# The head 0 preparation, one tile of the LRU products and the copies of the meta query's scores, moved in a hybrid encoder block on one core

## The reference

```
h = concat(meta (16 tokens), x (1024 tokens))            # T = 1040, D = 1024
proj = rmsnorm(h) @ w_in                                 # x_lru 512, g_lru 512, c_q 256, c_kv 128, k_pe 32
y_lru = rg_lru_bidir(dwconv(x_lru)) * gelu(g_lru)
q, k, v from c_q, c_kv, k_pe                             # 8 heads, QK = 96, V = 64, rmsnorm and rope
y_mla = softmax(q k^T / sqrt(96)) v                      # all 1040 keys
h = h + concat(rmsnorm(y_lru), rmsnorm(y_mla)) @ w_out
h = h + (silu(dwconv(gate)) * up) @ w_ffn_down           # gate, up = rmsnorm(h) @ w_ffn_up, D_FF = 2816
return h[:, 16:]
```

## Time and profile before

| what | value |
|---|---|
| median of 3 runs | 1298.33 us (1298.2 to 1304.07) |
| the profiled execution's own time | 1303.02 us |
| its span | 1301.2 us |
| TensorE busy | 1271.2 us, 98% of the span |
| VectorE busy | 996.9 us, 77% |
| ScalarE busy | 769.3 us, 59% |
| chain that ended last, by engine | PE 85%, DVE 6%, ACT 5%, issue 2%, DMA 1% |

### The profile page before, as it was taken

One profiled execution on the slowest core, in us unless ns is written; L12 is line 12 of the kernel. 1 busy time (PEld: TensorE's weight loads), 2 busy tenths in 40 slices (PEclk: granted clock), 3 DMA queues, 4 the chain that ended last, 5 costly groups with the idle time before them and its releaser, 6 DMA issues.

```text
span 1301.2 us, 18506 instructions
## 1 busy us (share of the span) xinstructions
PE 1271.2 (98%) x6158; PEld 1018.6 (78%) x6158; DVE 996.9 (77%) x1505; ACT 769.3 (59%) x1156; POOL 146.6 (11%) x175
## 2 busy tenths in 40 slices
PE   7999999899999999999999999999999999999998
PEld 7999997666666666687678888888888888888886
DVE  6677569678887876577779887887878887887855
ACT  7487648567765866534445565656474565656460
POOL 3000037400000001322200000000010000000010
PEclk9999999999999999999999999999999999999999
DMA  6111200000000014200144846576574847576667
GB/s 220 34 53 41 74 1 1 1 1 10 9 9 10 9 58 155 69 30 1 49 148 94 187 100 166 118 169 134 151 169 93 189 97 169 113 170 133 157 143 245
DMA packets 40938, 123.01 MB, mean 95 GB/s; under 512 B 7378, under 2 KB 8082, under 8 KB 34484
## 3 DMA queue, kind: packets, MB, share of 16 engines
q0 software_dynamic: 7200, 52.43, 21.4%
q1 hardware_dynamic: 33684, 69.86, 15.7%
HBM read 62.34 MB, written 59.80 MB: 94 GB/s over the span
## 4 chain that ended last, share of the span: by engine, by line
PE 85%; DVE 6%; ACT 5%; issue 2%; DMA 1%; POOL 0%; SPq 0%; DVEq 0%; ACTq 0%
PE banks L2911 30%; PE banks L2983 14%; PE banks L100 7%; PE banks L102 7%; PE banks L101 7%; PE banks L1935 2%; PE banks L2040 2%; PE banks L2041 2%; PE banks L2042 2%; PE banks L2060 2%; PE banks L2063 2%; PE banks L2061 2%; ACT e_f L1558 1%; PE banks L1895 1%; ACT e_h L1565 1%
## 5 line engine op out<-in xcount | busy, mean ns | idle before, releaser
L2911 PE MATMUL banks<-x_hi,slot_h 128*128 128x512 f32 x616 | 242.8, 394 | 2.5 <-DVE slot_l L2599 1.3
L2911 PE MATMUL banks<-x_lo,slot_h 128*128 128x512 f32 x616 | 243.4, 395 | 0.0
L2911 PE MATMUL banks<-x_hi,slot_l 128*128 128x512 f32 x616 | 242.9, 394 | 0.0
L2384 ACT ACTIVATE slot_h<-up_raw 128x512 fp32r<-128x512 f32 x127 | 79.8, 629 | 174.4 <-PE banks L2911 172.3
L2911 PEld LDWEIGHTS banks<-x_hi,slot_h 128*128 128x128 f32 x616 | 115.6, 188 | 30.9 <-DVE slot_l L2599 2.1
L2911 PEld LDWEIGHTS banks<-x_lo,slot_h 128*128 128x128 f32 x616 | 115.7, 188 | 27.1
L2911 PEld LDWEIGHTS banks<-x_hi,slot_l 128*128 128x128 f32 x616 | 115.7, 188 | 26.9
L2462 ACT ACTIVATE staged<-banks 128x1024 f32<-128x1024 f32 x100 | 101.4, 1026 | 41.0 <-PE banks L2983 41.0
L2983 PE MATMUL banks<-dn_h,a_h 128*128 128x512 f32 x280 | 110.4, 394 | 0.0
L2983 PE MATMUL banks<-dn_h,a_l 128*128 128x512 f32 x280 | 109.5, 391 | 0.0
L2983 PE MATMUL banks<-dn_l,a_h 128*128 128x512 f32 x280 | 109.5, 391 | 0.0
(11 more groups left out here) (346 smaller groups left out, 2861.5 us busy)
## 6 DMA issues: line engine op xcount, KB each, us to landing
down_sums<-staged POOLq DMA_DIRECT2D x50, 1024.0 KB, 8.0
...
```

The source lines that it names most:

```text
L2384: nc.scalar.activation(s_h[slot], x, ACT.Copy).then_inc(sem["up_hi"], 1)
L2911: ins = nc.tensor.matmul(o, s[slot][:, k], xs[w], start=fresh and k == 0 and n == 0, stop=k == 3 and n == 2, skip_group_check=not fresh)
```

## The change

- **Head 0's jobs.** `FIRST` packs the 23 jobs ahead of slot 0 in six steps, in a new order (`tq0`, `tk0`, `tq1`, `tk1`, `a0` to `a7`, and only then `tm`). They get eight banks by a list (`side_banks`). Each job waits only for the token tiles it reads (`HEAD_0`). The identity matmuls come ahead of a job and not behind it, and their numbers change: 1 at each of `a0` to `a15` becomes 2 from `a2` on, 6 at `a0`; 10 behind `tk0` become 10 spread over the four transposes; 8 behind `am` become 2 ahead of `r`.
- **Slots 0 and 1 of head 0.** `scores_ahead` computes the scores of both without the row of maxima, and adds the row's product as four matmuls of one row once it has come. In the two slots, where the pv of later slots stands, `keep_busy(8)` issues identity matmuls, 8 for each half.
- **Meta query.** VectorE copies `x0`, `x1`, `x2` out of PSUM, and ScalarE does not. In heads 0 to 6 they stand in slots 1, 2 and 4 (for head 0 they were ahead of slot 0, for heads 1 to 6 in slots 1, 1 and 2); those of head 7 move from slots 4, 5 and 6 of head 6 to slots 5, 6 and 8. SyncE issues `x_one` to `x_all` behind `recip_row` instead of ahead of it, in heads 0 to 6.
- **LRU tile.** The products of tile 4 run between the last pv of full key tiles and the meta pv of head 7. VectorE adds tile 4 ahead of two splits of weights, tile 5 ahead of two others, and tile 6 behind the multiplication of head 7's output; ScalarE splits tiles 6 and 7 earlier.

```diff
     LAST_AHEAD = dict(PREPARE)
-    LAST_AHEAD.update({4: ("a5", "x0", "a6", "a7"), 5: ("a8", "x1", "a9", "a10"), 6: ("a11", "x2", "a12", "a13")})
-    FIRST = dict(PREPARE)
-    FIRST.update({8: ("x0", "x1", "x2", "")})
-    OWN = {1: ("", "", "x0", "x1"), 2: ("", "x2", "", "")}
+    LAST_AHEAD.update({5: ("a8", "x0", "a9", "a10"), 6: ("a11", "x1", "a12", "a13"), 8: ("x2", "", "", "")})
+    FIRST = {0: ("tq0", "tk0", "tq1", "tk1"), 1: ("a0", "a1", "a2", "a3"), 2: ("a4", "a5", "a6", "a7"),
+             3: ("tm", "a8", "a9", "a10"), 4: ("a11", "a12", "a13", "a14"), 5: ("a15", "am", "r", "")}
+    OWN = {1: ("", "", "x0", ""), 2: ("", "x1", "", ""), 4: ("", "x2", "", "")}
...
             if h:
                 recip_row(sp, h - 1)
+            if h != END:
+                last_queries()
...
             if h == HEADS and s == 2:
+                split_y("L", 6)
                 read_output(h)
...
             if (h, s) == (HEADS, 1):
+                add_lru(L_GAP)
                 split_w(4)
                 split_w(5)
-                add_lru(4)
...
+            elif kind in ("x0", "x1", "x2"):
...
+                if c == 0:
+                    if h:
+                        dve.wait_ge(sem["x_in"], 16 * h)
...
+                ins = nc.vector.tensor_copy(x_one[:, 512 * c:512 * c + w], side[0:2, 0:w])
...
-        WARM = {"tk0": 10, "am": 8}
-        WARM.update({f"a{n}": 1 for n in range(2 * XT)})
+        WARM = {"tq0": 2, "tk0": 2, "tq1": 4, "tk1": 2, "a0": 6, "r": 2}
+        WARM.update({f"a{n}": 2 for n in range(2, 2 * XT)})
...
+        def scores_ahead():
+
+            pe.wait_ge(sem["b_set"], 2 + len(LOWS))
+            for g in range(2):
+                ks = slice(P * g, P * g + P)
+                for c in range(2):
+                    cs = slice(512 * c, 512 * c + 512)
+                    out = s_ps(g)[:, cs]
+                    nc.tensor.matmul(out, k_h[0][0:QK, ks], q_h[0][0:QK, cs], start=True, stop=False)
+                    nc.tensor.matmul(out, k_h[0][0:QK, ks], q_l[0][:, cs], start=False, stop=False)
+                    nc.tensor.matmul(out, k_l[0][:, ks], q_h[0][0:QK, cs], start=False, stop=False)
+            pe.wait_ge(sem["row_in"], 16)
+            for g in range(2):
+                for c in range(2):
+                    cs = slice(512 * c, 512 * c + 512)
+                    ins = nc.tensor.matmul(s_ps(g)[:, cs], k_h[0][QK:QK + 1, P * g:P * g + P], q_h[0][QK:QK + 1, cs],
+                                           start=False, stop=True)
+                ins.then_inc(sem["s_done"], 1)
+
+        def keep_busy(n):
+
+            for _ in range(n):
+                nc.tensor.matmul(bank(5)[:, 0:P], ident, ident, start=True, stop=True)
...
             for c in range(2):
-                if 0 <= g < G:
+                if 2 <= g < G:
                     scores(g, c)
                 place_job(h, s, js, c)
+            if g - 2 == G - 1:
+                for k in range(LF):
+                    lru_products(L_GAP, k)
             for c in range(2):
                 if 0 <= g - 2 < G:
                     pv(g - 2, c)
+                elif 0 <= g < 2:
+                    keep_busy(8)
                 place_job(h, s, js, 2 + c)
```

More of the change, by code:

```diff
@@ L1093, in side_jobs @@
         for plan, head in [(ahead, h + 1), (META_QUERIES, h), (LRU_SUMS, h), (OWN, h)]:
-            if plan is OWN and not 1 <= h < END:
+            if plan is OWN and not 0 <= h < END:
                 continue
@@ L1106, in attention_out_phase @@
     first = len([j for s in range(SLOTS) for j in side_jobs(-1, s) if j])
-    BY_ACT = {"r", "x0", "x1", "x2"}
-    LOWS = [("tq0", 0), ("tq1", 0), ("tk0", 0), ("tk1", 0)]
+    side_banks = [2, 3, 6, 7, 0, 1, 4, 5] + [(6, 7, 4, 5, 2, 3, 0, 1)[n % 8] for n in range(first - 9)] + [4] +\
+                 [6 + n % 2 for n in range(len(jobs) - first)]
+    BY_ACT = {"r"}
+    LOWS = [("tq0", 0), ("tk0", 0), ("tq1", 0), ("tk1", 0)]
     full = [place(f"qk_full{n}", WORDS - 8 - 512 * (n + 1), (512,), parts=QK) for n in range(len(LOWS))]
@@ L1118, in side_of @@
     def side_of(j):
-        n = number[j]
-        if n >= first - 3 and n < first:
-            return bank(4 + (n - first + 3) % 2, 1)
-        return bank([6, 7, 2, 3, 0, 1][n % 6] if n < first else 6 + (n - first) % 2, 1)
+        return bank(side_banks[number[j]], 1)
     def before(j):
         n = number[j]
-        if n < first - 3:
-            return jobs[n - 6:n - 5] if n >= 6 else []
-        if n < first:
-            return jobs[n - 2:n - 1] if n == first - 1 else []
-        return jobs[n - 2:n - 1] if n > first + 1 else [("r", 0), ("am", 0)]
+        return [i for i in jobs[:n] if side_banks[number[i]] == side_banks[n]][-1:]
+    FIRST_KEYS = [("a0", 0), ("a1", 0), ("a2", 0), ("a3", 0)]
     def hi_upto(j):
-        return sum(HIGH.get(i[0], 0) for i in jobs[:number[j]])
+        return 2 if j in FIRST_KEYS else sum(HIGH.get(i[0], 0) for i in jobs[:number[j]])
     def wait_read(eng, j):
@@ L1898, in tensor @@
     def tensor(pe):
-        WARM = {"tk0": 10, "am": 8}
-        WARM.update({f"a{n}": 1 for n in range(2 * XT)})
+        WARM = {"tq0": 2, "tk0": 2, "tq1": 4, "tk1": 2, "a0": 6, "r": 2}
+        WARM.update({f"a{n}": 2 for n in range(2, 2 * XT)})
+        HEAD_0 = {"tq0": (8, 4, 4, 0), "tk0": (8, 4, 4, 0), "a0": (NT, 0, 0, 0), "a1": (NT, 0, 0, 0),
+                  "tq1": (8, 8, 8, 0), "tk1": (8, 8, 8, 0)}
         def tile_of(i):
@@ L1910, in job @@
                 wait_read(pe, i)
-            if number[j] < 6 or j == ("tm", 0):
-                done = {"tq0": 8, "tq1": 8, "tk0": 8, "tk1": 8}.get(kind, NT)
-                pe.wait_ge(sem["q_scaled"], done)
-                pe.wait_ge(sem["kv_read"], done)
-                pe.wait_ge(sem["rope_done"], done)
-                pe.wait_ge(sem["v_full"], done)
+            if number[j] < 8 or j == ("tm", 0):
+                for name, done in zip(("q_scaled", "kv_read", "rope_done", "v_full"), HEAD_0.get(kind, (NT,) * 4)):
+                    if done:
+                        pe.wait_ge(sem[name], done)
+            if h == 0 and kind in WARM:
+                for _ in range(WARM[kind]):
+                    nc.tensor.matmul(side[:, 0:P], ident, ident, start=True, stop=True)
             if kind[:2] in ("tq", "tk"):
@@ L1965, in job @@
             ins.then_inc(sem["side_done"], 1)
-            if h == 0 and kind in WARM:
-                if kind == "a0":
-                    pe.wait_ge(sem["kv_read"], NT)
-                for _ in range(WARM[kind]):
-                    nc.tensor.matmul(bank(3 if kind == "tk0" else 5)[:, 0:P], ident, ident, start=True, stop=True)
         def meta_pv(s, i):
```

37 lines of the change are left out of this document (15 added, 22 removed).

## The result

The changed kernel takes 1311.77 us (1310.68 to 1312.14, 4 runs), against 1298.26 us (1297.1 to 1304.07, 4 runs) of the kernel before: ratio 1.0092, 95% interval [1.0076, 1.0108]. It is **slower by 0.9%, about 12 us** by the ratio; the two medians are 13.5 us apart. The forecast was 1300.6, range 1293.0 to 1307.0.

What follows compares the result with a forecast made beforehand. TensorE, busy 1271.2 of 1301.2 us, was taken to bound the kernel. The terms 3.7 − 2.4 + 2.3 + 2.0 − 3.3 = +2.3 us gave 1305.3 profiled, less 4.7 for the median: 1300.6 us, range 1293.0 to 1307.0.

Steps and rivals of the forecast that it cites:

- B: Starts of heads 1 to 6: k's low-part wait goes, o_sb comes later; −0.4 us per head, −2.4 us in all.
- Rival 2: VectorE's queue from x0 to o_sb bounds starts of heads 1 to 6: +0.8 us each, 1307.8 us; chance 0.12.
- D1: Head 6, slot 5: the copy of head 7's x0 waits for x_one's DMA behind recip_row; TensorE waits, +2.3 us.
- D2: Start of head 7: x2 is read later, so the row lands later and the first scores wait; +2.0 us.
- A: Head 0: r 2.1 us earlier, but 7.4 us of identity matmuls in slots 0 and 1; +3.7 us.
- F: End of the attention: tile 4 fills the wait for e_meta and the inversion runs earlier; −3.3 us.
- Carrying 4.7 us over: Last step: the median lay 4.7 us below the profiled execution, so 1305.3 became 1300.6 us.
- Rival 3: Half clock behind two new waits of some 2 us, 1.6 us each: 1303.8 us, with one 1302.2; chance 0.2.
- rival 1: Head 0's identity matmuls are free and the new waits absorbed: 1292.8 to 1294.8 us, at best 1288.4; chance 0.27.

Runs made afterwards that it cites:

- e4: Kernel before with the change's tail alone (LRU tile 4 ahead of the meta pv, tail work in the new order): ratio 0.9978, 1297.17 us.
- e7: Changed kernel with the whole meta query's part as in the kernel before, leaving the new head 0 and the tail: ratio 1.0002, 1299.92 us.
- e2: Changed kernel, but ScalarE copies x0, x1 and x2 out of PSUM as before: ratio 1.0011, 1302.06 us.
- e5: Kernel before, but VectorE instead of ScalarE copies x0, x1 and x2, in the old places: ratio 1.0043, 1305.12 us.
- e6: Changed kernel with VectorE's copy of x0 in heads 1 to 6 behind that of o_sb: ratio 1.0083, 1309.83 us.
- e10: Changed kernel with ScalarE's copies, x jobs of heads 6 and 7 in old places, no identity matmuls in slots 0 and 1: ratio 0.9994, 1299.98 us.
- e11: The kernel of e10 with the 32 identity matmuls back in slots 0 and 1 of head 0: ratio 0.9985, 1297.82 us.
- e12: Kernel before with the change's tail and new places of x0 to x2 in heads 1 to 5, ScalarE copying: ratio 0.9960, 1295.68 us.
- e1: Changed kernel without the 32 identity matmuls of slots 0 and 1 of head 0: ratio 1.0088, 1311.51 us.
- e14: Changed kernel with 16 identity matmuls instead of 8 at each of four places in head 0's slots 0 and 1: ratio 1.0150, 1319.26 us.

## Why the prediction was wrong

The three parts by ratios: tail −2.9 (e4), head 0 +3.1 (e7 less e4), meta query +11.7 us (the changed kernel less e7). They add up to the whole by the way they are taken, so their sum is no test.

In the profiled executions the forecast was +2.3 us and the span grew by 9.2. Of the 6.9 us between, heads 1 to 5 are 6.6 (−2.0 forecast, +4.6 measured), head 6 is 2.1 (+1.9, +4.0), head 0 0.7, head 7 −1.0, the tail −0.5 and the rest −0.9.

- **The step that failed is B.** The prediction gave −0.4 us to each of six heads; in the traces heads 1 to 5 came to +4.6 us, 1.0 of it a low clock (head 4 against heads 2 and 3). Rival 2 had the place (VectorE's queue from `x0` to `o_sb`) and about the size, 7.2 us over six heads. Its condition, `o_sb` over 0.7 us late, did not hold: TensorE waits 0.5 to 0.6 us for `o_sb`, and as long again in all for `k_l`. The forecast's range ended at 1307.0, below the 1307.8 of this rival. The working saw that `x0`'s copy goes ahead of `o_sb`, but stopped there: `k_l` of the next head is queued behind `o_sb`, and in heads 2 to 4 a sum of 1.22 us stands between. That row is in VectorE's timeline of the kernel before, and wasn't read:

```profile
320.14 1.21 DVE L1733 COPY o_sb<-banks 66x1024 f32<-66x1024 f32 x1
321.27 1.22 DVE L1643 TENSOR_TENSOR y_sum<-y_sum,y_sq 128x1026 f32<-128x1026 f32 x1
322.73 0.75 DVE L1147 SCALAR_TENSOR_TENSOR k_l<-banks,par,k_h 96x512 fp32r<-96x512 f32 x1 [0.23 <-ACT k_h L1433]
```

Only 0.23 us were free there, for a copy of 0.69. VectorE's 77% over the span was taken as evidence against; the queue in slot 1 is full. e2, e5 and e6 show it.
- **D1** was right in place and mechanism. The wait is 2.9 us (forecast 2.3), and the sum put the low clock behind it at nothing. With it D1 is 4.3 us in the traces, 5 to 7 in the medians. The DMA landed some 3 us after its issue; 2.4 were assumed.
- **D2** came as forecast, with 1.3 us instead of 2.0, and no cost that a median shows.
- **A** was +4.35 us where 3.7 were forecast: `r` is 1.2 us earlier and not 2.1; from the row to slot 3 it took the forecast's 14.8 us. In the medians it is 3.1. Two of its reasons were off. The filler hides 3.3 of its 7.2 us, and not behind ScalarE: without it TensorE waits 1.12 and 1.75 us for `q_l` of VectorE. And it is the reason in the traces, but taking it out doesn't mend the median (e10, e11). The traces say how that can be. `r_row` of head 1 is at 276.06 us before and at 275.19 in e12, both with the old head 0. With the new one it is at 275.47 without filler at full clock (e1), at 279.07 without filler and with the low stretch (e10), and at 279.52 with filler (e11). So the new order gains nothing even at its best: what the earlier row gives, the waits for `q_l` take. How often the low stretch comes without the filler is not shown.
- **F** was forecast at −3.3 us and measured −3.81 in the traces, −2.9 in the medians. The chain of DMAs is what is late next, as forecast.
- **Carrying 4.7 us over** from the profiled execution to the median was unsound. That execution ran at a mean granted clock of 0.993. Of 19 runs of the kernel before beside e1 to e4, two at 0.993 took 1302.7 us on average and two at 1.000 took 1298.7. The changed kernel's profiled execution was no slow one of its kind: it is 0.4 us above its median. So 9.1 us between profiled executions (1312.14 less 1303.02) became 13.5 between medians, 12 by the ratio. Its four runs were all at or below a clock of 0.996, but so were 14 of those 19, so they show no change of the usual clock.
- **Rival 3** (low clock behind the new waits) had 0.2, and half of it came true. The wait of 2.9 us had a low stretch behind it and that of 1.3 had none. One more followed the waits of 0.52 and 0.82 us at the start of head 4; the same waits at heads 2 and 3 had none. Between 225 and 560 us the 14 profiled executions have seven waits of TensorE of 2.7 us or more: at D1 in the changed kernel, e1, e2, e6 and e14, and at the meta pv in before and e5. All seven had a low clock behind them. The Trainium skill, "TensorE: Matmul & The Clock Gate", section "HAM oscillation — how this bites in real kernels", puts the slow bursts of its example down to the engine's wait for a DMA ahead of each. The traces agree at D1, where the copy of `x0` waited for a DMA, in five of five; shorter waits gave both outcomes. The old head 0 has a wait of 1.4 us for `k_h` (1.40 us in the earlier trace rows); before and e4 had a low clock behind it, e5 and e12 had none. With the new head 0 it is so for e1 and e10.
- A slip in rival 1: both waits absorbed and B at its best add up to −9.6 us, not −9.9. It changes nothing.

The prices agree with rows now: the Trainium skill, "VectorE: DVE Perf Modes", section "The TRN2 errata", makes it an estimated 0.66 us on VectorE and 0.57 on ScalarE for a 512-column copy out of PSUM, and the traces have 0.68 and 0.58. What made the move dear was not this 0.1 us but what stood behind it.

Open: the parts don't add within the meta query. Undoing the copies alone gives 10.5 us and mending D1 alone 7.0, more than the 11.7 of the whole, which has in it a gain of some 2.3 from the new places (e12 against e4), if that gain is real. The intervals (about 2 us for a difference) and the clock can make this up, but no run shows it.
